# A fused two-block transformer kernel: causal attention restricted to the keys that each half of the queries can see, and two stages' weighted activations moved from SBUF to PSUM

## The reference, cut to what matters

```python
def _causal_softmax(logits, q_pos, k_pos):
    mask = k_pos[None, :] <= q_pos[:, None]
    logits = jnp.where(mask, logits.astype(jnp.float32), -1e30)
    return jax.nn.softmax(logits, axis=-1)
...
        s = jnp.einsum('bqhd,bkhd->bhqk', qb, k) * scale
        p = _causal_softmax(s, q_pos, pos)
        return jnp.einsum('bhqk,bkhd->bqhd', p.astype(v.dtype), v)
...
        s_own = s_own - sl * rel.astype(jnp.float32)
        s_own = jnp.where(rel >= 0, s_own, -jnp.inf)
...
        act = jax.nn.gelu(jnp.einsum('cd,chkd->chk', xc, u_sel).astype(jnp.float32), approximate=False)
        v_sel = jnp.take(v, experts, axis=0)
        return jnp.einsum('chk,chkd->cd', (g * act).astype(v.dtype), v_sel)
...
    return (jax.nn.silu(a) * g) @ w_down
```

## Time and profile before

| what | value |
|---|---|
| time, median of 3 runs | 1487.13 us (1483.68 to 1488.05) |
| the profiled execution's own time | 1484.81 us |
| its span | 1483.0 us |
| mean granted TensorE clock | 0.975 of 2.4 GHz |
| TensorE busy | 1428.3 us, 96% |
| VectorE / ScalarE / POOL busy | 1001.3 / 684.2 / 541.5 us |
| chain that ended last: TensorE / VectorE / ScalarE | 91% / 6% / 1% |

### The profile page before, as it was taken

How to read it: one execution, slowest core, us unless ns; L and a number is a source line. 1 busy time by engine, 2 the same in 40 slices (tenths; PEclk the granted TensorE clock), 3 DMA queues, 4 the chain that set the end, 5 groups by cost and what they waited for, 6 DMA issues and landing times.

```text
span 1483.0 us, 31411 instructions
## 1 busy us (share of the span) xinstructions
PE 1428.3 (96%) x11038; PEld 1348.1 (91%) x11038; DVE 1001.3 (68%) x2085; ACT 684.2 (46%) x1035; POOL 541.5 (37%) x252
## 2 busy tenths in 40 slices
PE   6999988999999999999999999999999998999997
PEld 5776668999999999999999999999989867899997
DVE  4524544889788888877676766665655745599997
ACT  4433644445555555543333333444464345545553
POOL 2313227778500000034444443444423335254541
PEclk9999989999999999999999999999999978999999
DMA  7420125666755555567777777555643504255552
GB/s 280 131 71 31 42 86 179 192 192 206 232 177 175 175 177 177 174 193 230 236 230 233 233 229 225 176 189 178 187 173 115 174 25 132 86 185 185 183 181 74
DMA packets 89994, 250.16 MB, mean 169 GB/s; under 512 B 10048, under 2 KB 35920, under 8 KB 89296
## 3 DMA queue, kind: packets, MB, share of 16 engines
q1 hardware_dynamic: 86112, 238.20, 50.9%
q10 hardware_dynamic: 3824, 11.17, 2.0%
HBM read 234.09 MB, written 15.24 MB: 168 GB/s over the span
## 4 chain that ended last, share of the span: by engine, by line
PE 91%; DVE 6%; ACT 1%; issue 1%; DMA 0%; POOL 0%; ACTq 0%; DVEq 0%
PE ps L1652 46%; PE ps L2028 28%; PE ps L2011 4%; PE ps L1916 2%; PE ps L1870 2%; PE ps L1667 1%; PE ps L1890 1%; PE ps L1841 1%; DVE big L1070 1%; DVE w_lo L1048 1%; PE ps L1731 1%; PE ps L1984 0%; PE ps L1762 0%; ACT w_hi L594 0%; DVE big L1062 0%
## 5 line engine op out<-in xcount | busy, mean ns | idle before, releaser
L493 POOL TENSOR_TENSOR w_lo<-raw,w_hi 128x1024 fp32r<-128x1024 f32 x193 | 489.0, 2535 | 810.2 <-ACT w_hi L594 810.1
L1652 PE MATMUL ps<-x_op,w_hi 128*128 128x256 f32 (+1 forms) x3968 | 744.4, 289 | 15.5 <-DVE x_op L1066 8.8
L1652 PEld LDWEIGHTS ps<-x_op,w_hi 128*128 128x128 f32 x3968 | 624.2, 193 | 27.5 <-issue 20.5
L1652 PE MATMUL ps<-x_op,w_lo 128*128 128x256 f32 (+1 forms) x1984 | 565.4, 285 | 0.0
L594 ACT ACTIVATE w_hi<-raw 128x1024 fp32r<-128x1024 f32 x400 | 420.5, 1055 | 266.2 <-PE ps L2028 214.3
L2028 PE MATMUL ps<-h_op,w_hi 128*128 128x256 f32 x2400 | 426.8, 279 | 2.4 <-DVE h_op L1602 2.4
L1652 PEld LDWEIGHTS ps<-x_op,w_lo 128*128 128x128 f32 x1984 | 383.4, 193 | 0.0
L2028 PEld LDWEIGHTS ps<-h_op,w_hi 128*128 128x128 f32 x2400 | 367.8, 188 | 3.1 <-issue 1.8
L1048 DVE TENSOR_TENSOR w_lo<-raw,w_hi 128x1024 fp32r<-128x1024 f32 x207 | 265.2, 1281 | 120.6 <-ACT w_hi L594 120.4
L2028 PE MATMUL ps<-h_op,w_lo 128*128 128x256 f32 x1200 | 337.2, 281 | 0.0
L2028 PEld LDWEIGHTS ps<-h_op,w_lo 128*128 128x128 f32 x1200 | 225.2, 188 | 0.0
(11 more groups left out here) (268 smaller groups left out, 1040.5 us busy)
## 6 DMA issues: line engine op xcount, KB each, us to landing
raw<-blocks SPq DMA_DIRECT2D x404, 512.0 KB, 3.6
early_store<-kv_mem SPq DMA_DIRECT2D x96, 128.0 KB, 1.7
work<-early_store SPq DMA_DIRECT2D x96, 128.0 KB, 3.6
big<-consts ACTq DMA_DIRECT2D x2, 1336.0 KB, 6.8
big<-h_t ACTq DMA_DIRECT2D x4, 272.0 KB, 3.7
big<-bias_lines ACTq DMA_DIRECT2D x8, 136.0 KB, 2.7
bias_lines<-route_t ACTq DMA_DIRECT2D x4, 264.0 KB, 3.1
res<-mem_t SPq DMA_DIRECT2D x1, 1024.0 KB, 8.2
```

What stands on the lines that cost most here:

```text
L493: pool.tensor_tensor(w_lo[:, s, :], raw[:, s, :], w_hi[:, s, :].bitcast(F32), ALU.subtract).then_inc(sem("lo_pool"), 1)
L1652: mm = pe.matmul(ps[:, m_bank, 0:T], w, x, start=(k == 0 and j == 0), stop=(k == last and j == 2))
```

## The change

Causal units work on fewer keys. `seen(u, t)` is the number of keys that half t can see: for 272 keys 144 and 272, for MoBA's 256 keys 128 and 256, for the memory attention always all 256. Scores, mask or bias, maximum, exponential, normalise and combine run per half on that many columns; where one instruction covered both halves (maximum, MoBA's distance term, POOL's multiply) there are now two. `key_tiles` yields for each tile of 128 keys the first query that sees it, rounded down to a multiple of 32, and where its columns lie in a packed row: for 272 keys 256 + 160 + 32 = 448 columns, for MoBA 256 + 128 = 384, for the memory 512. All tiles lie in bank 6; the transposes take only the rows from that query on, the copy to `probs_t` is one of 448, 384 or 512 columns, and the values product of a tile accumulates into the queries that see it. The transposes of units with 272 keys no longer wait for the output bank. Columns 144 to 255 of the first half are set to zero once by POOL, since a transposed tile still reads some of them. `hf` becomes a view of PSUM banks 2 and 3; the multiply writes there, and the copy and the subtract read from there.

```diff
@@ -187,7 +187,7 @@
         scores_sb = area(3, 2, NK)
-        probs_t = area(2, 3, NQ)
+        probs_t = area(2, 2 * NQ)
         row_max = area(3, 2)
@@ -294,7 +294,7 @@
         ge = work[:, 0].rearrange("p a b c -> p a (b c)")[:, :, 0:NQ]
-        hf = work[:, 1].rearrange("p a b c -> p a (b c)")[:, :, 0:NQ]
+        hf = ps[:, 2:4, 0:NQ]
         a_in = work[:, :].rearrange("p w a b c -> p (w a) (b c)")[:, :, NQ:2 * NQ]
@@ -374,6 +374,25 @@
+        def seen(u, t):
+            keys = units[u]["keys"]
+            return keys if units[u]["kind"] == "xattn" else min(keys, keys - NQ + P * (t + 1))
+        def key_tiles(u):
+            at = 0
+            for j in range(-(-units[u]["keys"] // P)):
+                if units[u]["kind"] == "xattn":
+                    first = 0
+                else:
+                    first = max(0, P * j - (units[u]["keys"] - NQ)) // 32 * 32
+                yield j, min(P, units[u]["keys"] - P * j), first, at
+                at += NQ - first
+        def probs_width(u):
+            return sum(NQ - first for _, _, first, _ in key_tiles(u))
         def memory_bank(j):
@@ -522,13 +541,14 @@
                 for u in range(a, b):
-                    x, n = units[u], units[u]["keys"]
+                    x = units[u]
                     if x["kind"] == "diff" and x["map"] == 1:
                         continue
-                    s = scores_sb[:, u % 3, :, 0:n]
                     pool.wait_ge(sem("row_inverse"), u + 1)
-                    pool.tensor_tensor(s, s, row_inv[:, u % 3, :].unsqueeze(2).to_broadcast([P, 2, n]), ALU.mult
-                                       ).then_inc(sem("probs_normed"), 1)
+                    for t in range(2):
+                        s = scores_sb[:, u % 3, t, 0:seen(u, t)]
+                        ins = pool.tensor_tensor(s, s, row_inv[:, u % 3, t:t + 1].to_broadcast([P, seen(u, t)]), ALU.mult)
+                    ins.then_inc(sem("probs_normed"), 1)
@@ -554,6 +574,10 @@
                 ALU.add).then_inc(sem("bias_ready"), 1)
+            pool.wait_ge(sem("q_sum"), 1)
+            pool.wait_ge(sem("k_sum"), 2)
+            pool.memset(scores_sb[:, :, 0, P + N_META:2 * P], 0.0)
             normalise(U_MLA, U_MOBA)
@@ -775,10 +799,10 @@
-                n = units[u]["keys"]
                 act.wait_ge(sem("max_ready"), u + 1)
                 kind, h = units[u]["kind"], units[u]["head"]
                 for t in range(2):
+                    n = seen(u, t)
                     s = scores_sb[:, u % 3, t, 0:n]
@@ -787,11 +811,10 @@
-                x, o = units[u], units[u]["out"]
+                o = units[u]["out"]
                 act.wait_ge(sem("probs_turned"), o + 1)
-                if x["keys"] > NQ:
-                    act.activation(probs_t[0:N_META, o % 2, 2, :], ps[0:N_META, out_bank(o), NQ:2 * NQ], ACT.Copy)
-                act.activation(flat2(probs_t[:, o % 2, 0:2, :]), ps[:, 6, :], ACT.Copy).then_inc(sem("probs_ready"), 1)
+                n = probs_width(u)
+                act.activation(probs_t[:, o % 2, 0:n], ps[:, 6, 0:n], ACT.Copy).then_inc(sem("probs_ready"), 1)
@@ -1187,9 +1210,9 @@
                 x = units[u]
-                n, b = x["keys"], 2 + 2 * (u % 2)
-                s = scores_sb[:, u % 3, :, 0:n]
-                src = ps[:, b:b + 2, 0:n]
+                b = 2 + 2 * (u % 2)
+                s = [scores_sb[:, u % 3, t, 0:seen(u, t)] for t in range(2)]
+                src = [ps[:, b + t, 0:seen(u, t)] for t in range(2)]
                 dve.wait_ge(sem("scores_done"), u + 1)
@@ -1202,7 +1225,7 @@
                     for t in range(2):
-                        ins = dve.tensor_tensor_reduce(s[:, t], src[:, t], mask[:, t], 1.0, -3.0e38, ALU.add, ALU.max, m[:, t:t + 1])
+                        ins = dve.tensor_tensor_reduce(s[t], src[t], mask[:, t, 0:seen(u, t)], 1.0, -3.0e38, ALU.add, ALU.max, m[:, t:t + 1])
                     ins.then_inc(sem("scores_read"), 1)
@@ -1213,19 +1236,22 @@
                     for t in range(2):
-                        ins = dve.scalar_tensor_tensor(out=s[:, t], in0=src[:, t], scalar=rq[:, 1, t, 2 * h + x["map"]:2 * h + x["map"] + 1],
-                                                       in1=bias[:, h, t], op0=ALU.mult, op1=ALU.add)
+                        ins = dve.scalar_tensor_tensor(out=s[t], in0=src[t], scalar=rq[:, 1, t, 2 * h + x["map"]:2 * h + x["map"] + 1],
+                                                       in1=bias[:, h, t, 0:seen(u, t)], op0=ALU.mult, op1=ALU.add)
                 elif x["kind"] == "moba":
                     rel = con("rel", at=cst2).rearrange("p (t k) -> p t k", t=2)
-                    ins = dve.scalar_tensor_tensor(out=s, in0=rel, scalar=2.0 ** (-8.0 * (h + 1) / MH), in1=src,
-                                                   op0=ALU.mult, op1=ALU.add)
+                    for t in range(2):
+                        ins = dve.scalar_tensor_tensor(out=s[t], in0=rel[:, t, 0:seen(u, t)], scalar=2.0 ** (-8.0 * (h + 1) / MH),
+                                                       in1=src[t], op0=ALU.mult, op1=ALU.add)
                 if x["kind"] == "xattn":
-                    s = src
+                    step(dve.tensor_reduce(m, ps[:, b:b + 2, 0:NQ], AX.X, ALU.max))
                 else:
                     ins.then_inc(sem("scores_read"), 1)
                     dve.wait_ge(sem("scores_read"), u + 1)
-                step(dve.tensor_reduce(m, s, AX.X, ALU.max))
+                    for t in range(2):
+                        ins = dve.tensor_reduce(m[:, t:t + 1], s[t], AX.X, ALU.max)
+                    step(ins)
                 dve.tensor_scalar(row_max[:, u % 3, :], m, -1.0, None, ALU.mult).then_inc(sem("max_ready"), 1)
@@ -1851,22 +1877,22 @@
                 x = units[u]
-                h, n, b = x["head"], x["keys"], 2 + 2 * (u % 2)
+                h, b = x["head"], 2 + 2 * (u % 2)
                 if u >= 2:
                     pe.wait_ge(sem("exp_done" if units[u - 2]["kind"] == "xattn" else "scores_read"), u - 1)
                 for t in range(2):
-                    c = slice(P * t, P * t + P)
+                    c, n = slice(P * t, P * t + P), seen(u, t)
                     half = slice(64 * (h % 2), 64 * (h % 2) + 64)
                     if x["kind"] == "mla":
-                        q, k = q_mla[:, h, c], k_mla[:, h, :]
+                        q, k = q_mla[:, h, c], k_mla[:, h, 0:n]
                     elif x["kind"] == "diff":
                         half = slice(64 * x["map"], 64 * x["map"] + 64)
-                        q, k = dqn[half, h, c], dkn[half, h, :]
+                        q, k = dqn[half, h, c], dkn[half, h, 0:n]
                     elif x["kind"] == "moba":
-                        q, k = proj2[half, 6 + h // 2, c], proj2[half, 10 + h // 2, :]
+                        q, k = proj2[half, 6 + h // 2, c], proj2[half, 10 + h // 2, 0:n]
                     else:
-                        q, k = q_x[half, h // 2, c], kv_x[half, h // 2, :]
+                        q, k = q_x[half, h // 2, c], kv_x[half, h // 2, 0:n]
                     mm = pe.matmul(ps[:, b + t, 0:n], q, k, start=True, stop=True)
@@ -1877,34 +1903,30 @@
-                o, n = units[u]["out"], units[u]["keys"]
+                o = units[u]["out"]
                 if o is None:
                     return
                 pe.wait_ge(sem("probs_normed"), u + 1)
                 if o:
                     pe.wait_ge(sem("probs_ready"), o)
-                if o >= 2 and n > NQ:
-                    outputs_out(o)
-                for t in range(2):
-                    for j in range(2):
-                        mm = pe.transpose(ps[:, 6, j * NQ + t * P:j * NQ + t * P + P], scores_sb[:, u % 3, t, j * P:j * P + P], ident)
-                    if n > NQ:
-                        mm = pe.transpose(ps[0:N_META, out_bank(o), NQ + t * P:NQ + t * P + P], scores_sb[:, u % 3, t, NQ:n], ident)
+                for j, k, first, at in key_tiles(u):
+                    for t in range(first // P, 2):
+                        r = max(first - P * t, 0)
+                        a = at + P * t + r - first
+                        mm = pe.transpose(ps[0:k, 6, a:a + P - r], scores_sb[r:P, u % 3, t, P * j:P * j + k], ident[r:P, r:P])
                 mm.then_inc(sem("probs_turned"), 1)
             def weigh(u):
                 x = units[u]
-                o, h, n = x["out"], x["head"], x["keys"]
+                o, h = x["out"], x["head"]
                 if o is None:
                     return
                 pe.wait_ge(sem("probs_ready"), o + 1)
                 if o >= 2:
                     outputs_out(o)
                 rows = slice(0, P) if x["kind"] == "diff" else slice(64 * (h % 2), 64 * (h % 2) + 64)
-                tiles = 3 if n > NQ else 2
-                for t in range(tiles):
-                    k = min(P, n - P * t)
+                for t, k, first, at in key_tiles(u):
                     if x["kind"] == "mla":
```

(3 more changed lines are left out.)

## The result

The changed kernel takes **1499.74 us** (median of 5 runs, 1496.97 to 1502.01) against 1487.11 for the kernel before on the same chip: a ratio of 1.0089, 95% interval 1.0074 to 1.0104. The forecast was 1474.8 us, range 1468.5 to 1482.5, so the kernel got slower where faster was forecast, and its time lies outside the range. The profiled execution has a span of 1500.2 us, 17.2 more than before.

What follows compares the result with a forecast made beforehand. TensorE was taken to bound the expert, feed-forward and most attention stretches, VectorE the differential heads. Parts -6.7 - 1.4 - 1.1 - 3.6 + 0.5 = -12.3 from 1484.8, plus 2.3, gave 1474.8 us, range 1468.5 to 1482.5.

Steps and rivals of the forecast that it cites:

- part E: Expert sums and feed-forward products in PSUM: longer copies hidden except in four stage-edge tiles; +0.5 us, bounds 0 and +1.0.
- the slower rival: First attention: with fewer columns the clock falls to 1.2 GHz; 1501 us with all ten MLA units low; chance 0.05.
- a feed-forward tile over 8.6 us: Feed-forward stage: a tile of 72 matmuls longer than this was named as a sign that the forecast is wrong.
- Part A: MLA units, 139 to 178 us: narrower scores, values and transposes, 2.59 us a unit for 3.38; -6.7, bounds -3.6 and -8.4.
- the bound of +0.19: MLA transposes: one saved, but two starting at partition 96 expose 0.15 us each, nothing for width; the forecast took -0.10.
- Rival 2: Attention: turnaround eats the columns, a unit is 3.0 us instead of 2.59; total 1479.6 us, chance 0.17.
- rival 4: First attention: the clock falls as fewer columns may not hold it; an MLA unit then costs 5.2 us; chance 0.05.
- B: VectorE-led differential heads: shorter bias steps and combines, less ScalarE work before the last unit; -1.4 us, bounds -0.9 and -2.2.
- C: Tail of the differential heads: less ScalarE work, shorter values product and transposes, partly lost to the clock; -1.1 us, bounds -0.7 and -1.9.
- Part D: MoBA, 1184 to 1215 us: unit 3.87 us at 1.2 GHz for 4.95, clock rising after 15.4 us; -3.6, bounds +3.7 and -5.5.
- rival 1: MoBA: the clock stays at 1.2 GHz through its units, D = +3.7 us; total 1482.1 us, chance 0.18.
- The second rule: VectorE copy and subtract: 62 cycles more for a PSUM source than SBUF; E would be +1.1 us, not used in the sum.

Runs made afterwards that it cites:

- e_ffn_sb: The whole change, but with the feed-forward stage's activations in SBUF as before and those of the expert sums in PSUM; 1485.43 us, ratio 0.9997 to the kernel before.
- e_attn: The attention part of the change alone, with the weighted activations left in SBUF; 1491.39 us, ratio 1.004 to the kernel before.
- e_dummy3: The kernel before, all in SBUF, plus a VectorE memset of 224 columns ahead of its second w_lo subtraction of a feed-forward tile; 1494.42 us, ratio 1.0049.
- e_psum: The PSUM line of the change alone, put into the kernel before with its old attention; 1496.89 us, ratio 1.008.
- e_pool_late: The whole change plus one 96-column POOL instruction ahead of each of POOL's feed-forward w_lo subtractions; 1485.87 us, ratio 0.9996 to the kernel before.
- e_pool_late2: The whole change plus a 16-column POOL instruction ahead of each of POOL's feed-forward w_lo subtractions; 1484.96 us, ratio 0.9994 to the kernel before.

## Why the prediction was wrong

The forecast was -12.3 us and the change made +12.6, a miss of some 25 in two halves. Parts A to D were forecast at -12.8 and came to -0.8 (`e_ffn_sb` against the kernel before, with PSUM in the expert sums); part E was forecast at +0.5 and came to about +14.

**The step that failed: part E**, "Hidden in all tiles but those at the stage edges". The size of the copy was right, 0.424 us for a forecast of 0.42. What I took for cover was TensorE's solid stretch; I had VectorE at 147.77 of 164.00 us and called the rest slack. I never asked who else uses the 0.13 us. Between VectorE and POOL these passes exclude each other, the margin by which VectorE came first at the stage's start was 0.01 us (w_lo at 1307.83 on VectorE and 1307.84 on POOL in the trace of before; 0.57 once the good order had settled, as at 1410), and the price of losing it is 2.1 us in every pair of tiles. I had the sign in front of me: the 128 copies ranged to 1.194 us, and I wrote that the excess "may go, off the path". I read that row as a loss to be saved and not as two engines taking turns, which can also change who waits. E was put at +0.5, bounds 0 and +1.0; it measured about +14, by `e_ffn_sb` against the change. None of the five rivals was this one; the slower rival was about the clock. The text did name the right sign, a feed-forward tile over 8.6 us; it is 9.4.

**Part A** was mis-sized in one term of the gain. The unit measured 2.90 for 2.59. The kernel before's own chain, at units with no memory block between, reads

```profile
163.73 1.11 PE ps L1870 x4
164.84 1.58 PE ps L1916 x6
```

and 0.81 of transposes, 3.50 in all; the 0.92 of the earlier trace rows stands behind a block, and I took it for the rule. Scores went from 1.11 to 0.90 (-0.21, forecast -0.22), values from 1.58 to 1.07 (-0.51, forecast -0.47), transposes from 0.81 to 0.93: +0.12 where I had -0.10. In all a unit gained 0.60 for 0.79. Five transposes took longer than six; the bound of +0.19 was the value to take. Here the page "TensorE: Matmul & The Clock Gate" of the Trainium skill was cited, section "LDWEIGHTS (loading the stationary operand)", with the rule that a load's time goes by columns and not by rows. On the load itself the trace agrees: 135 ns for 32 rows and 128 columns, 140 for 128 rows, though both are longer than the 107 of the page's formula.

```profile
L1916 PEld LDWEIGHTS ps<-kept,big 128*128 128x128 f32 x21 | 2.4, 140 | 0.9 <-issue 0.4
L1916 PEld LDWEIGHTS ps<-kept,big 32*128 32x128 f32 x7 | 0.9, 135 | 1.2 <-issue 1.2
```

The sum that I drew from it, 0.60 for a unit's transposes, is not what happened: the 1.2 us of idle ahead of the seven narrow loads are 0.17 each, about the 0.15 that the bound went by. Rival 2 (unit 3.0) was nearest.

**Parts A to C, the clock.** The first attention lost it from 142 to 150 and from 186 to 208; before, from 196 to 206 alone. This is rival 4 in part, which I gave 0.05. What the units gained went there: 0.6 us is left of 9.2. B and C can't be told apart from it without fills.

**Part D** went as rival 1 in the clock: unit sizes right to 0.01 us, clock 0.50 from 1188 to 1215. In time it went as neither: from its first scores to the next stage's first product MoBA took 33.1 us for 32.8 before (1185.1 to 1218.2, 1183.0 to 1215.8), +0.3 where I had -3.6 and rival 1 had +3.7. I took the clock to return after the same 15.4 us as before; nothing in the trace bound me to that. What I missed is that the clock is the larger lever. It fell with TensorE idle for 3 us at the stage's start, in the kernel before too, and 3 us of matmuls there are worth 9 us.

**The second rule**, from the Trainium skill's page "VectorE: DVE Perf Modes", section "The TRN2 errata — SBUF-src ops pay a fixed extra latency per instruction", was read as 62 cycles more on the copy and on the subtraction. By the page's figures the copy would take an estimated 0.20 us more; it takes 0.13. The subtraction with one input in PSUM and one in SBUF takes 424 ns, with both in SBUF 426: no difference. By it E would have been an estimated +1.1, as far from +14 as my own number.

Three readings in the prediction are off without effect on this. The clock's fall lies at 1185.70 and not at 1185.85 (a mean of 0.85 over the microsecond from 1185 is 0.3 us at half speed). The probability copy of 0.52 fits beside scores of 0.70 by 0.18, not 0.1. And half of 1.5 us is 0.75; C was put at -1.1, between that and the whole.

What stays open: why the attention part alone (`e_attn`) shifts the expert sums so that six subtractions fall behind POOL's pass; it wasn't tried whether a shift by some tenths of a microsecond undoes it. Nor do the runs separate two things that PSUM changes in the feed-forward tile: the copy is 0.13 us longer, and copy and subtraction no longer contend with POOL, so that POOL can start under them. `e_dummy3` shows that a delay alone is enough for the loss, but it doesn't hold the bad order through the stage as `e_psum` does. And how long the clock's fall lasts was changed, but not measured against the amount of fill.

## What to carry to other kernels

Where two engines take turns at a common access, slack is not additive: before calling an added tenth of a microsecond hidden, look in the timeline for the other engine's pass that starts within a few tenths of it, and price the case in which the order turns. A row whose longest is several times its median is where to look. Where work is taken from TensorE, look at its granted clock first; idle time ahead of light matmuls can cost more than the matmuls, and filling it with dummy work paid here: 9 to 10 us with the narrowed units, some 2 us for all fills in the kernel before.

## What the runs showed of the hardware

**A VectorE pass with one of its inputs in PSUM isn't held by POOL.** The subtraction of the expert sums, with its product in PSUM (changed kernel) and in SBUF (kernel before), min, median and max of 128:

```profile
L1429 DVE TENSOR_TENSOR h_op<-ps,h_op x128: 423/424/426, 642.8 to 1082.3; 128x256 fp32r<-128x256 f32 x128
```

```profile
L1403 DVE TENSOR_TENSOR h_op<-work,h_op x128: 424/426/2680, 640.6 to 1080.1; 128x256 fp32r<-128x256 f32 x128
```

The copy shows the same: 423 to 426 ns from PSUM in all 128, 293 to 1194 from SBUF. So the copy loses 0.13 us and gains freedom from POOL. The place of the output doesn't matter: the gate product writes to PSUM in the change, reads two SBUF tensors, and takes 2.63 us at 1412.20, 0.43 where POOL is not in its way (`e_pool_late`). In `e_pool_late2` the subtraction at 1408.89 runs in 0.42 us inside POOL's pass, and the w_lo at 1409.24, with both inputs in SBUF, is held. It is this that makes PSUM worth 6.0 us in the expert sums of the narrowed kernel, where six subtractions from SBUF are held in `e_attn` and none from PSUM in `e_ffn_sb`.

**One kernel can hold two steady states of the same loop**, 17.1 and 18.75 us for two tiles, and `e_dummy3` moved between them in one execution.

**The clock's level outlives its cause.** With the narrowed MoBA units' matmuls (64 rows or 64 columns, and transposes), nearly back to back (25.28 of 27.00 us), it stayed at 0.50 behind the idle 3.09 us; with the same matmuls and 2.2 of 10 us idle it stayed at 1.00, once it stood there. It doesn't last for ever: in the kernel before it rose within the MoBA units, at about 1202.8.
